# A hybrid decoder trunk: differential queries turned by VectorE and device memory, and two insertions moved

## The reference

```
h = RMSNorm(x)
pool | diff q,k,v | stick-breaking q,k,v | forgetting q,k,v | forget logits | gate logits = h @ w_in
x = x + (sum over four branches of sigmoid(gate) * (branch output @ w_branch)) @ w_out
x = x + SwiGLU(RMSNorm(x))
```

```
q = rope(rms_norm(q, q_gain));  k = rope(rms_norm(k, k_gain))
weights = softmax(q1 k1 * 64**-0.5) - lam * softmax(q2 k2 * 64**-0.5)
o = rms_norm(weights @ v, subln_gain) * (1 - lambda_init)
```

## Time and profile before

| | us |
|---|---|
| median of three executions | 849.31 |
| the profiled execution, own time | 849.36 |
| its span, first to last instruction | 847.6 |
| TensorE busy in the span | 842.3 |
| VectorE, ScalarE, GpSimd busy | 605.3, 445.5, 114.9 |
| TensorE's share of the chain that ended last | 99% |
| TensorE's waits for other engines, in total | 2.6 in 4 waits |

### The profile page before, as it was taken

The page is one execution under the profiler, slowest core; times in us unless marked ns, Lnnn a source line. Parts: engine busy times, 40 slices in busy tenths (PEclk is TensorE's granted clock), DMA queues, the critical chain, the costliest instruction groups (busy, mean ns, idle before and its releaser), DMA issues.

```text
span 847.6 us, 11122 instructions
## 1 busy us (share of the span) xinstructions
PE 842.3 (99%) x4126; PEld 699.2 (83%) x4126; DVE 605.3 (71%) x890; ACT 445.5 (53%) x650; POOL 114.9 (14%) x89
## 2 busy tenths in 40 slices
PE   9999999999999999999999999999999999999998
PEld 7888888888888888888888888888888888888887
DVE  7885977679677666665479668868687776666643
ACT  6657645754454455444365675557543644444431
POOL 0750201004502000000005402010054000000000
PEclk9999999999999999999999999999999999999999
DMA  9846666477567777666566365764965577666651
GB/s 340 286 164 179 200 214 192 148 243 232 184 199 244 203 220 218 202 218 217 173 185 191 109 191 172 237 202 123 296 189 169 177 236 205 205 202 220 222 188 50
DMA packets 100934, 170.43 MB, mean 201 GB/s; under 512 B 12944, under 2 KB 26768, under 8 KB 100880
## 3 DMA queue, kind: packets, MB, share of 16 engines
q1 hardware_dynamic: 100448, 169.07, 63.8%
q10 hardware_dynamic: 432, 0.66, 0.3%
HBM read 160.77 MB, written 3.15 MB: 193 GB/s over the span
## 4 chain that ended last, share of the span: by engine, by line
PE 99%; DMA 1%; ACT 0%; issue 0%; DVE 0%; ACTq 0%
PE bulk L1761 30%; PE bulk L1765 30%; PE bulk L1762 30%; PE bankAB L1526 2%; DMA raw<-in_w_in_dram 1%; PE bankT L1673 0%; PE bulk L1808 0%; PE bankAB L1662 0%; PE bulk L1789 0%; PE bankAB L1620 0%; PE bulk L1795 0%; PE bankAB L1535 0%; PE bankO L1631 0%; PE bankO L1683 0%; PE bankO L1691 0%; PE bankO L1685 0%
## 5 line engine op out<-in xcount | busy, mean ns | idle before, releaser
L1087 DVE TENSOR_TENSOR w_lo<-raw,w_hi 128x1024 fp32r<-128x1024 f32 (+1 forms) x288 | 360.2, 1268 | 116.9 <-ACT w_hi L812 114.4
L812 ACT ACTIVATE w_hi<-raw 128x1024 fp32r<-128x1024 f32 (+1 forms) x286 | 295.5, 1047 | 206.7 <-PE bulk L1765 202.6
L1761 PE MATMUL bulk<-w_hi,hT_hi 128*128 128x512 f32 (+1 forms) x880 | 342.8, 390 | 0.0
L1762 PE MATMUL bulk<-w_lo,hT_hi 128*128 128x512 f32 (+1 forms) x880 | 339.3, 386 | 0.0
L1765 PE MATMUL bulk<-w_hi,hT_lo 128*128 128x512 f32 (+1 forms) x880 | 336.3, 386 | 0.0
L1761 PEld LDWEIGHTS bulk<-w_hi,hT_hi 128*128 128x128 f32 x880 | 165.3, 188 | 33.1 <-issue 0.5
L1765 PEld LDWEIGHTS bulk<-w_hi,hT_lo 128*128 128x128 f32 x880 | 165.0, 188 | 33.3
L1762 PEld LDWEIGHTS bulk<-w_lo,hT_hi 128*128 128x128 f32 x880 | 165.4, 188 | 32.0
L1761 PE MATMUL bulk<-w_hi,aT_hi 128*128 128x512 f32 x174 | 67.8, 390 | 0.0
L1765 PE MATMUL bulk<-w_hi,aT_lo 128*128 128x512 f32 x174 | 67.7, 389 | 0.0
L1762 PE MATMUL bulk<-w_lo,aT_hi 128*128 128x512 f32 x174 | 67.7, 389 | 0.0
(11 more groups left out here) (239 smaller groups left out, 715.6 us busy)
## 6 DMA issues: line engine op xcount, KB each, us to landing
raw<-in_w_in_dram SPq DMA_DIRECT2D x110, 512.0 KB, 4.5
raw<-in_w_ffn_up_dram SPq DMA_DIRECT2D x80, 512.0 KB, 4.1
raw<-in_w_ffn_down_dram SPq DMA_DIRECT2D x44, 512.0 KB, 3.6
raw<-in_w_branch_dram SPq DMA_DIRECT2D x20, 512.0 KB, 5.3
raw<-in_w_out_dram SPq DMA_DIRECT2D x16, 512.0 KB, 3.3
wide<-wide SPq DMA_DIRECT2D x160, 32.0 KB, 2.7
bias<-in_b_gate_dram SPq DMA_DIRECT2D x16, 256.0 KB, 4.9
raw<-in_w_ffn_up_dram SPq DMA_DIRECT2D x16, 256.0 KB, 3.4
```

The lines of the kernel that those rows point to most:

```text
L812: act.activation(w_hi[:, g % RING, :, 0:width], raw[:, g % RAW, :, 0:width], ACT.Copy).then_inc(hi_ready, 1)
L1087: vec.tensor_tensor(w_lo[:, g % RING, :, 0:width], raw[:, g % RAW, :, 0:width], w_hi[:, g % RING, :, 0:width].bitcast(F32), ALU.subtract). ...
L1761: pe.matmul(dst, hi, whi, start=(k == ks[0]), stop=False)
L1762: pe.matmul(dst, hi, wlo, start=False, stop=False)
```

## The change

1. `dq` joins `TURN_AT` (step 13) and `BY_DRAM`: VectorE turns the rotated queries with two block transposes, SyncE sends them to device memory and back, both at its unit 17. `tr_qk` of `dq` at slot 14 goes. `qk_evac` of `dq` moves from step 15 to 19 and reads SBUF.
2. The factor 64^-0.5 of the queries goes into the gain on GpSimd, ahead of the rotation tables; the evacuations no longer multiply.
3. `tr_forget` moves on TensorE from slot 39 to slot 37, and `forget_evac` from step 39 to 37, ahead of the softmax of head 3.
4. `pv` of head 2 moves from slot 39 to slot 42, ahead of `tr_probs` of head 3. `pv_evac` of head 2 moves on VectorE from step 39 to step 42, behind `softmax` of fox 0.
5. `turn` of `diff` moves from step 49 to 48, and its DMAs with it.
6. Buffers: `fox_gained` stands ahead of `o_d`; `probs_diff` and `probsT` become parts of one `probs_room`; the queries are turned through `o_d` and `probs_room`.

```diff
 MIXING_PE = [
-    (9, "tr_ss"), (14, "tr_qk", "dq"), (14, "sb_scores", 0), (18, "sb_sums", 0), ...
+    (9, "tr_ss"), (14, "sb_scores", 0), (18, "sb_sums", 0), ...
-    (37, "scores", "diff", 3), (37, "pv", "diff", 1), (39, "tr_probs", "diff", 2), (39, "pv", "diff", 2), (39, "tr_forget"), (42, "tr_probs", "diff", 3), (42, "scores", "fox", 0), (42, "pv", "diff", 3),
+    (37, "scores", "diff", 3), (37, "pv", "diff", 1), (37, "tr_forget"), (39, "tr_probs", "diff", 2), (42, "pv", "diff", 2), (42, "tr_probs", "diff", 3), (42, "scores", "fox", 0), (42, "pv", "diff", 3),
-TURN_AT = {"fox": 33, "diff": 49}
+TURN_AT = {"dq": 13, "fox": 33, "diff": 48}
-BY_DRAM = ('fox', 'diff')
+BY_DRAM = ('dq', 'fox', 'diff')
+for _s in ('dq',):
+    SPREAD_AT.setdefault(TURN_AT[_s] + AHEAD, []).extend([(_s, "out"), (_s, "back")])
 MIXING_ACT = [
-    ... (15, "qk_evac", "dq"), ... (39, "forget_evac"), ...
+    ... (19, "svfq"), (19, "qk_evac", "dq"), ... (37, "probs_evac", "diff", 1), (37, "forget_evac"), (38, "softmax", "diff", 3), ...
 MIXING_DVE = [
-    ... (15, "qk_evac", "dq"), (19, "sb_mask", 1), ... (39, "pv_evac", "diff", 2), (39, "softmax", "diff", 3), ...
-    (41, "maxima", "fox", 0), (41, "softmax", "fox", 0), (42, "pv_evac", "diff", 3), ...
+    (13, "turn", "dq"), ... (19, "sb_mask", 1), (19, "qk_evac", "dq"), ... (39, "softmax", "diff", 3), ...
+    (41, "maxima", "fox", 0), (41, "softmax", "fox", 0), (42, "pv_evac", "diff", 2), (42, "pv_evac", "diff", 3), ...
+    ... (48, "diff_norm"), (48, "pv_evac", "fox", 0), (48, "turn", "diff"), (49, "softmax", "fox", 1), ...
 def qk_evac(layer, which):      # VectorE
-    vec.scalar_tensor_tensor(out=low, in0=bank[...], scalar=HD ** -0.5 if which == "dq" else 1.0, in1=high, ...)
+    src = spread_columns(which, t, (0, 4)) if which in TURN_AT else bank[...]
+    vec.tensor_tensor(low, src, high.bitcast(F32), ALU.subtract).then_inc(qkT_ready, 1)
```

More of the change, by code:

```diff
@@ L132 @@
 MIXING_PE = [
-    (9, "tr_ss"), (14, "tr_qk", "dq"), (14, "sb_scores", 0), (18, "sb_sums", 0), (20, "sb_out", 0), (20, "sb_scores", 1),
-    (23, "sb_sums", 1), (24, "tr_qk", "dk"), (25, "sb_out", 1), (25, "scores", "diff", 0), (30, "tr_probs", "diff", 0),
-    (30, "scores", "diff", 1), (30, "pv", "diff", 0), (35, "cum"), (35, "scores", "diff", 2), (35, "tr_probs", "diff", 1),
-    (37, "scores", "diff", 3), (37, "pv", "diff", 1), (39, "tr_probs", "diff", 2), (39, "pv", "diff", 2), (39, "tr_forget"), (42, "tr_probs", "diff", 3), (42, "scores", "fox", 0), (42, "pv", "diff", 3),
-    (47, "tr_probs", "fox", 0), (47, "scores", "fox", 1), (47, "pool_a"), (47, "pv", "fox", 0), (50, "pool_b"),
-    (52, "tr_probs", "fox", 1), (56, "pv", "fox", 1), (68, "tr_merged", 0),
+    (9, "tr_ss"), (14, "sb_scores", 0), (18, "sb_sums", 0), (20, "sb_out", 0), (20, "sb_scores", 1), (23, "sb_sums", 1),
+    (24, "tr_qk", "dk"), (25, "sb_out", 1), (25, "scores", "diff", 0), (30, "tr_probs", "diff", 0), (30, "scores", "diff", 1),
+    (30, "pv", "diff", 0), (35, "cum"), (35, "scores", "diff", 2), (35, "tr_probs", "diff", 1), (37, "scores", "diff", 3),
+    (37, "pv", "diff", 1), (37, "tr_forget"), (39, "tr_probs", "diff", 2), (42, "pv", "diff", 2), (42, "tr_probs", "diff", 3),
+    (42, "scores", "fox", 0), (42, "pv", "diff", 3), (47, "tr_probs", "fox", 0), (47, "scores", "fox", 1), (47, "pool_a"),
+    (47, "pv", "fox", 0), (50, "pool_b"), (52, "tr_probs", "fox", 1), (56, "pv", "fox", 1), (68, "tr_merged", 0),
     (73, "tr_merged", 1)]
@@ L209 @@
     (4, "qk_norm", "dq"), (8, "ss"), (10, "ss_evac"), (11, "lambda_sums"), (14, "qk_norm", "dk"), (14, "sb_logs", 0),
-    (14, "sb_split", 0), (15, "qk_evac", "dq"), (16, "sb_weights", 0), (19, "svfq"), (20, "sb_logs", 1), (21, "sb_split", 1),
+    (14, "sb_split", 0), (16, "sb_weights", 0), (19, "svfq"), (19, "qk_evac", "dq"), (20, "sb_logs", 1), (21, "sb_split", 1),
     (21, "sb_evac", 0), (21, "fkfv"), (22, "sb_weights", 1), (24, "qk_evac", "dk"), (25, "sb_evac", 1), (25, "dv"),
     (27, "softmax", "diff", 0), (29, "probs_evac", "diff", 0), (30, "pf"), (30, "fox_forget"), (32, "softmax", "diff", 1),
-    (36, "softmax", "diff", 2), (37, "probs_evac", "diff", 1), (38, "softmax", "diff", 3), (38, "probs_evac", "diff", 2),
-    (39, "forget_evac"), (39, "fox_evac", "fq"), (39, "fox_evac", "fk"), (41, "probs_evac", "diff", 3),
+    (36, "softmax", "diff", 2), (37, "probs_evac", "diff", 1), (37, "forget_evac"), (38, "softmax", "diff", 3),
+    (38, "probs_evac", "diff", 2), (39, "fox_evac", "fq"), (39, "fox_evac", "fk"), (41, "probs_evac", "diff", 3),
     (42, "softmax", "fox", 0), (46, "sigmoid", 0, 0), (46, "probs_evac", "fox", 0), (48, "softmax", "fox", 1),
@@ L222 @@
     (3, "qk_sums", "dq"), (5, "row_mean"), (5, "qk_norm", "dq"), (7, "lambda_sums"), (7, "ss_evac"), (10, "lambdas"),
[L223 to L231, removed]
@@ L232 @@
-    (57, "pv_evac", "fox", 1), (60, "gate", 7), (69, "merged_evac", 0), (71, "merged_evac", 1)]
+    (13, "turn", "dq"), (14, "qk_norm", "dk"), (14, "sb_mask", 0), (14, "sb_split", 0), (19, "sb_mask", 1),
+    (19, "qk_evac", "dq"), (20, "sb_split", 1), (22, "sb_evac", 0), (24, "qk_evac", "dk"), (25, "sb_evac", 1),
+    (25, "maxima", "diff", 0), (27, "softmax", "diff", 0), (29, "pf"), (29, "fox_norm"), (29, "fox_forget"),
+    (30, "maxima", "diff", 1), (30, "pv_evac", "diff", 0), (32, "softmax", "diff", 1), (32, "gate", 0), (32, "cum_evac"),
@@ new lines @@
+    (33, "maxima", "diff", 2), (33, "turn", "fox"), (36, "gate", 1), (37, "softmax", "diff", 2), (37, "maxima", "diff", 3),
+    (37, "pv_evac", "diff", 1), (39, "softmax", "diff", 3), (39, "fox_evac", "fq"), (39, "fox_evac", "fk"), (40, "gate", 2),
+    (41, "maxima", "fox", 0), (41, "softmax", "fox", 0), (42, "pv_evac", "diff", 2), (42, "pv_evac", "diff", 3),
+    (44, "gate", 3), (47, "maxima", "fox", 1), (48, "diff_norm"), (48, "pv_evac", "fox", 0), (48, "turn", "diff"),
+    (49, "softmax", "fox", 1), (49, "gate", 4), (49, "pool_evac_b"), (52, "gate", 5), (55, "diff_evac", 1),
@@ L236, in evacuations @@
+    (55, "diff_evac", 0), (56, "gate", 6), (57, "pv_evac", "fox", 1), (60, "gate", 7), (69, "merged_evac", 0),
+    (71, "merged_evac", 1)]
 def evacuations(mixing, *branches):
@@ L399, in build @@
         v_d = sb("v_d", [P, TT, 512], F32, mixing)
+        fox_gained = sb("fox_gained", [P, TT, 512], F32, mixing)
+        foxes = {"fq": fox_gained[:, :, 0:256], "fk": fox_gained[:, :, 256:512]}
         o_d = sb("o_d", [P, TT, 4, P], F32, mixing)
@@ L402, in build @@
         v_f = sb("v_f", [P, TT, 256], F32, mixing)
-        fox_gained = sb("fox_gained", [P, TT, 512], F32, mixing)
-        foxes = {"fq": fox_gained[:, :, 0:256], "fk": fox_gained[:, :, 256:512]}
         forget_rows = sb("forget_rows", [P, P + 16], F32, mixing)
@@ L414, in build @@
         expd = sb2
-        probs_diff = sb("probs_diff", [P, 384], F32, mixing)
+        probs_room = sb("probs_room", [P, 1152], F32, mixing)
+        probs_diff = probs_room[:, 0:384]
         probs_of = {"diff": [probs_diff[:, :]], "fox": [sb1[:, 0, :], sb1[:, 1, :]]}
-        probsT = sb("probsT", [P, 2, 384], F32, mixing)
+        probsT = probs_room[:, 384:1152].rearrange("p (i q) -> p i q", i=2)
         mixing.close()
@@ L454, in build @@
         normed_place = (quads(wide[:, 0, 0:D]), quads(wide[:, 1, 0:D]))
+        unused = (quads(o_d[:, :, :, :].rearrange("p t h d -> p (t h d)")), quads(probs_room[:, 0:D]))
         def turning(stage):
@@ L459, in turning @@
             blocks = FF_BLOCKS[stage[1]] if kind == "act" else 4
-            return (*{"act": normed_place, "dq": late, "diff": late}.get(kind, early), blocks)
+            return (*{"act": normed_place, "dq": unused, "dk": unused, "diff": late, "merged": late}.get(kind, early), blocks)
         def spread_columns(stage, t, blocks):
@@ L732, in _ @@
                 pool.wait_ge(params_loaded, 16 * (layer + 1))
+                pool.tensor_scalar(gains[:, 0:3:2, :], gains[:, 0:3:2, :], HD ** -0.5, None, ALU.mult).then_inc(pool_step, 1)
+                pool.wait_ge(pool_step, count_step())
                 for i in range(2):
@@ L737, in _ @@
                     last = pool.tensor_tensor(ropeB[:, i, :, half:HD], sin[:, :, half:HD], g[:, :, 0:half], ALU.mult)
-                last = pool.tensor_scalar(gains[:, 2, :], gains[:, 2, :], HD ** -0.5, None, ALU.mult)
                 last.then_inc(tables_ready, 1)
@@ L874, in qk_evac @@
             def qk_evac(layer, which):
+                if which in TURN_AT:
+                    wait_spread(act, layer, which)
                 for t in range(TT):
[L876 to L879, removed]
+                    if which in TURN_AT:
+                        src = spread_columns(which, t, (0, 4))
+                    else:
+                        act.wait_ge(stage_done, nth(stage_done, layer, ("tr_qk", which, t)))
+                        src = bank[QK_BANKS[which][t]].rearrange("p (h g q) -> p h g q", h=4, g=NQUAD)
```

(11 more changed lines are left out.)

## The result

The changed kernel takes 864.45 us (median of 4 runs, 863.50 to 864.52) against 849.22 before: ratio 1.0177, 95% interval 1.0159 to 1.0195. Forecast were 860.8, in 857.5 to 864.3; the median lies 0.15 us above that end.

The account below looks back on a forecast made before the run. TensorE, busy 842.3 of 847.6 us, was taken to bound the kernel. 849.36 - 1.74 - 1.48 + 11.93 + 0.89 = 858.96, plus 1.85 for the clock, gave 860.8 us, range 857.5 to 864.3.

Parts of the forecast that it names:

- no transposes at slot 14, two layers: Slot 14: TensorE drops the eight query transposes, 0.87 us a layer; gain 1.74 us, bounds 1.6 and 1.9.
- layer 0 waits in slots 16 to 18: Layer 0, slot 18: unit 18 waits 0.89 us for its split, delayed by the queries' turn; bounds 0 and 1.3.
- wait at slot 39 gone: Slot 39: head 2's value products no longer wait for their evacuation; gain 1.48 us, bounds 1.2 and 1.7.
- stand at slot 42, two layers: Slot 42: head 3's value products wait for VectorE's copy of head 2, behind fox 0's softmax; 11.93 us together.
- lower clock behind it: Behind the slot 42 stands: TensorE's clock falls at one of the two, taken as 1.85 us of 0 to 3.7.
- The rival on the other side: Slot 42: TensorE doesn't wait, so the kernel gets faster, 847.0 us; chance 0.04.
- a fall costs between 0 and 1.85 us each: Behind each slot 42 stand: loss from a clock fall, its upper end taken from the warm-up matmuls.
- the rival that said so: Slot 42: the clock falls at both stands, adding 3.7 us, 862.7 us in all; chance 0.30.
- The warm-up row: Kernel's start: 35 slow warm-up matmuls, 3.7 us at the lower clock level, read as a loss of 1.85 us.
- The round trip: Layer 0: queries return from device memory by about 61.6 us, before ScalarE's work at 63.28; cost 0.
- GpSimd's factor: GpSimd, ahead of the rotation: the gain's factor replaces an instruction of the same kind; cost 0.
- the turn of `diff`: Step 48: the earlier turn delays fox 1's softmax by some 1.2 us; cost 0, at worst 0.5 a layer.

Follow-up runs that it names:

- e2: Changed kernel with only the queries' part kept, the other moves put back: 849.38 us, ratio 1.0002 to the kernel before.
- e8: Kernel before with only the moves, queries still transposed on TensorE, head 2's copy ahead of maxima of fox 0: 847.40 us, ratio 0.9979.
- e4: Changed kernel with 30 matmuls nobody reads on TensorE ahead of the wait for bank O at slot 42: 859.93 us, ratio 1.0127.
- e1: Changed kernel with VectorE's copy of head 2 ahead of maxima of fox 0 instead of behind its softmax: 847.59 us, ratio 0.9982.
- e5: Changed kernel with VectorE's copy of head 2 between maxima and softmax of fox 0: 853.32 us, ratio 1.0046.
- e9: e1 with the queries' turn at step 15, their evacuation at 22, and the mask casts at step 9 instead of 12: 846.51 us, ratio 0.9968.

## Why the prediction was right, and what was mis-sized

The terms of the sum, and what each measured:

| term | forecast | measured | by |
|---|---|---|---|
| no transposes at slot 14, two layers | -1.74 | } +0.20 together | e2 |
| layer 0 waits in slots 16 to 18 | +0.89 | } | |
| wait at slot 39 gone | -1.48 | -1.83 | e8 |
| stand at slot 42, two layers | +11.93 | +12.34 | e4 less e1 |
| lower clock behind it | +1.85 | +4.52 | after less e4 |
| sum | +11.45 | +15.23 | |

- **The stand** was the mechanism, the place and the size: a wait behind a chain that TensorE itself starts. It came out 0.2 us a layer above; 0.1 of it is the restart, which I had only in the bounds. The rival on the other side (faster, 847.0) fell, and e1 (847.59) is what it would have been. The measured parts add up: e2 and e8 together give 849.2 + 0.20 - 1.83 = 847.6, which is e1. So the two halves of the change don't interact, and the earlier turn of `diff`, which of these three e1 alone has, costs nothing that shows.
- **The clock** is the term that was mis-sized, and most of the error (2.7 of 3.8 us). The step that failed: "a fall costs between 0 and 1.85 us each", taken as one fall of two; it is why the time lies above my range. Both stands brought it, so the rival that said so was right in kind and, with 862.7, nearer than my forecast, and each fall cost 2.3 us (4.52 for two), above the end that I took from the warm-up. The warm-up row measures half rate from a first matmul at the kernel's start; it is no upper bound for a stretch elsewhere (5.2 us of low clock behind the restart in the changed kernel, against the 3.7 of the warm-up). I also read the 1.00 of the earlier trace rows as a sign that the column may not show such a fall. In the middle of the kernel it does. The changed kernel, in both layers, agrees with what I cited of the Trainium skill, page "TensorE: Matmul & The Clock Gate", section "HAM oscillation — how this bites in real kernels": TensorE found its clock halved when it resumed. Not every stand does it: behind the one of 2.1 us in layer 1 of e5 the clock stayed at 1.00.
- **Layer 0's loss** was named at the wrong slot and too small. "TensorE waits 0.83 + 0.06 = 0.89 us" at unit 18 rests on the split of its weights; I had followed what VectorE delivers, `softplus_lo` and `w_lo`, and not what its instructions release. The bank of `bulk` that unit 16 takes is released by the keys' normalising, which is in the same delayed chain and comes first. Its cover was 0.6 us, against 0.8 + 1.0 taken from it and 0.1 for the restart: 1.38 us (53.60 - 52.22) at that slot, and in e2 half a microsecond more of slot 14's gain goes into the wait for the masks (e9 moves that wait, and gains nothing). In all the queries' part, with its turn at step 13, brings nothing.
- **Slot 39**: forecast 0.74 a layer, measured 0.9. The start behind a wait is itself slower (124.58 to the next at 124.90, 0.32 us against 0.22 elsewhere), and so it is at slot 16 in the changed kernel (53.60 to 53.91) and behind the wait in e4 (142.00 to 142.33).
- **The round trip, GpSimd's factor, `forget_evac` and the turn of `diff`** cost nothing that any profile here shows as a wait of TensorE. The last three weren't tried one by one.

What stays open: what sets the moment of the fall (1.3 to 4.2 us into the stand, and in e5 0.4 us behind the restart), and why the same 2.1 us stand brings it in one layer and not in the other. The experiments show that it varies, not by what rule.

## What to carry to other kernels

When the producer of a buffer moves in one engine's order, look up where its consumer stands in the others' and what that consumer will be queued behind; if that is work which the waiting engine starts itself at the same place, the whole chain is laid on it. A copy that frees a bank belongs ahead of any wait for later results. And for every instruction that gets delayed, list what it releases (banks, buffers) beside what it delivers.

## What the runs showed that I had not expected

TensorE's clock can fall to half behind a stand of 2.1 us (e5, layer 0; not layer 1), and work after it runs at half rate for 3 to 5 us, less when the fall comes early in the stand. In the changed kernel this added 2.3 us a stand to 6.2 us of standing. Thirty matmuls that nobody reads, 5.0 us of a 5.9 us wait, kept it at full rate and paid back 4.5 us (e4).
